# Sparse attention with a fused score step, late normalisation and value products 64 columns wide

## Chip, cores and metric

One NeuronCore of one Trainium2 chip runs the whole program. The metric is the time of one execution on the device, in microseconds. The kernel before was timed three times: 2421.4, 2422.6 and 2425.72 us, median 2422.6 us.

## The reference, cut to what matters

The program is a stack of transformer layers over 256 tokens of width 1024, all in fp32: feed-forward blocks, a convolution mixer, a sparse-attention mixer, and then two further layers with differential and grouped-query attention. The change touches the sparse-attention mixer alone (`nsa_mixer`). It has 16 heads of 64 in 4 groups, and three branches: compressed keys (15 of them), selected blocks and a window. With 256 tokens there are only 4 blocks of 64, and all are selected; the window of 512 holds all keys too. So every branch is a masked softmax over the visible keys, with a distance penalty that has a slope for each head:

```python
def masked_softmax(s, mask):
    s = jnp.where(mask, s, NEG_INF)
    m = jnp.max(s, axis=-1, keepdims=True)
    e = jnp.where(mask, jnp.exp(s - m), 0.0)
    return e / jnp.maximum(jnp.sum(e, axis=-1, keepdims=True), 1e-30)

s = jnp.einsum('bqgrd,bgnd->bgrqn', qb, k_cmp) - sl5 * d_cmp      # likewise for k_sel and kw
p_cmp = masked_softmax(s, d_cmp >= 0)
o_cmp = jnp.einsum('bgrqn,bgnd->bqgrd', p_cmp, v_cmp)
o = gates[0] * o_cmp + gates[1] * o_sel + gates[2] * o_win        # gates = sigmoid(projection)
```

## The kernel before, in words

Each engine has one hand-ordered program, and semaphores join them. Large weight matrices are split into a high and a low fp32r part (`split`, L636 and L1027) and multiplied in three passes. The sparse-attention mixer comes as one of eleven stages, between two feed-forward stages. It has three parts. First four weight units give the queries (`cols_product`) and a narrow one the gates. Then comes the attention loop. Then `down` (L1599) multiplies the result `mid[:, 0:2048]` by the output matrix, in four steps, each of which needs a slice of the result that `mid_split` has split in two (L648 on ScalarE, L1035 on VectorE).

The attention loop runs over `nsa_jobs` (L257): 24 jobs, for each of 4 groups `g`, each of 2 tiles `tt` of 128 queries, and the branches 1, 2 and 0 in that order. A job treats 4 heads together. Its number of keys `nk` is 128 for tile 0 and 256 for tile 1, and 15 in branch 0. Two successive tiles of one group make six jobs, called a pair of tiles below. A job passes through these steps, where J is the loop's step on each engine:

- TensorE, `nsa_pe` (L1739): scores of job J (L1767, 4 products, each two fp32 instructions), into banks 0 and 1 or 2 and 3; transposes of the probabilities of job J-2 (L1779), into bank 4 and, for 256 keys, bank 5; value products of job J-3 (L1789, L1792): the values are the stationary operand, the transposed probabilities of all 4 heads the moving one, 512 columns. The three branches add up in one bank.
- VectorE, `nsa_dve` (L1234): for job J the biased scores (L1256, one instruction for each head), their maximum (L1259), its negation (L1261); then for job J-1 the denominator (L1272 and L1274 only in branch 0, L1276), its reciprocal (L1278), times the gate (L1281), and the product of all probabilities with it (L1284).
- ScalarE, `nsa_act` (L811): the exponentials of job J (L827, one for each head, each with a sum that is read out by a second instruction), the copy of job J-2's transposed probabilities from the banks to `pT` (L835, L838), and for a finished tile the copy of the output (L845, L846).

The probabilities have two buffers, `probs[J % 2]`, and the transposes have one set of banks. VectorE's L1256 of job J waits for the transposes of job J-2 (L1252), which wait for L1284 of job J-2 and for the copy of job J-3. At the loop's end TensorE waits for the last output copies (L1795, L1796).

## Time and profile before

| | |
|---|---|
| median of three executions | 2422.6 us |
| the profiled execution | 2424.26 us |
| its span, first to last instruction | 2422.3 us |
| TensorE busy | 92% of the span |
| VectorE busy | 49% |
| ScalarE busy | 39% |
| mean granted TensorE clock | 0.948 of 2.4 GHz |
| attention loop, first score to first product of `down` | 968.6 to 1109.6 us |

Shares of the whole span are means over eleven stages. The loop is some 6% of the span, and has to be read by itself: with the busy times of a stretch, with the waits in it, and with the chain of work. "Idle before" is the time for which an engine stood still ahead of an instruction, and the name behind the arrow is what released it. A granted clock of 1.00 is 2.4 GHz, and 0.50 is 1.2 GHz.

### The profile page before, as it was taken

The page shows a single profiled execution, that of the slowest core. Times are in us where ns is not written, and L with a number is a line of the kernel's source. Part 1 is how long each engine was busy: PE and PEld are TensorE (multiplying, and loading weights), DVE is VectorE, ACT ScalarE, POOL GpSimd, SP SyncE. Part 2 cuts the span into 40 slices and gives each one's busy share as a digit, 9 for nine tenths or more (in the row PEclk, how much of TensorE's full clock was granted, in tenths as well). Part 3 has the DMA queues.
Part 4 walks back from the last instruction along what each step waited for, and adds up shares of the span by engine and source line. Part 5 has one row for each costly group of instructions (what it writes and reads, how often), then busy time and mean ns, then how long its engine had stood idle before and what let it go on. Part 6 is the DMA issues. An engine that isn't in the chain of part 4 may idle for free.

```text
span 2422.3 us, 34862 instructions
## 1 busy us (share of the span) xinstructions
PE 2228.2 (92%) x14142; PEld 1868.5 (77%) x14142; DVE 1189.1 (49%) x1891; ACT 947.1 (39%) x1456; POOL 92.3 (4%) x140
## 2 busy tenths in 40 slices
PE   4999998999889998677999999788999999898999
PEld 2998786997789978335997799556877768786997
DVE  2344655445724455555445564785222233765454
ACT  2334424334523344445334543564222222455343
POOL 1000000000100000000000100002000000200000
PEclk7999998999969998678999999999999999999999
DMA  7876686767548674003776432002554333225553
GB/s 264 289 252 258 212 319 224 272 227 261 174 160 289 216 273 135 8 1 122 257 251 240 130 105 88 18 2 87 173 174 156 121 139 113 70 70 173 173 176 121
DMA packets 246601, 411.38 MB, mean 170 GB/s; under 512 B 10221, under 2 KB 191942, under 8 KB 246470
## 3 DMA queue, kind: packets, MB, share of 16 engines
q1 hardware_dynamic: 246470, 409.54, 48.8%
q8 instruction: 93, 1.52, 0.3%
q14 instruction: 38, 0.31, 0.0%
HBM read 408.47 MB, written 1.05 MB: 169 GB/s over the span
## 4 chain that ended last, share of the span: by engine, by line
PE 79%; DVE 9%; ACT 5%; DMA 3%; issue 2%; POOL 2%; SPq 0%; DVEq 0%; ACTq 0%; POOLq 0%
PE bank L1629 19%; PE bank L1577 14%; PE bank L1578 13%; PE bank L1579 13%; PE bank L1552 4%; PE bank L1686 3%; PE bank L1688 3%; PE bank L1687 3%; DMA ada<-in_ada_w 2%; ACT gate_b L827 1%; PE bank L1779 1%; PE bank L1720 1%; PE bank L1563 1%; PE bank L1597 1%; DVE astat L1373 1%
## 5 line engine op out<-in xcount | busy, mean ns | idle before, releaser
L1033 DVE TENSOR_TENSOR w_lo<-stage,w_hi 128x2048 fp32r<-128x2048 f32 x255 | 585.8, 2299 | 736.3 <-ACT w_hi L646 736.1
L1577 PE MATMUL bank<-h_hi,w_hi 128*128 128x256 f32 (+1 forms) x2432 | 742.9, 305 | 26.9 <-POOL h_lo L611 20.8
L1578 PE MATMUL bank<-h_lo,w_hi 128*128 128x256 f32 (+1 forms) x2432 | 733.5, 302 | 0.0
L1579 PE MATMUL bank<-h_hi,w_lo 128*128 128x256 f32 (+1 forms) x2432 | 733.2, 301 | 0.0
L646 ACT CAST w_hi<-stage 128x2048 fp32r<-128x2048 f32 x255 | 484.7, 1902 | 620.5 <-PE bank L1579 260.6
L1577 PEld LDWEIGHTS bank<-h_hi,w_hi 128*128 128x128 f32 x2432 | 473.4, 195 | 86.4 <-issue 69.5
L1578 PEld LDWEIGHTS bank<-h_lo,w_hi 128*128 128x128 f32 x2432 | 473.6, 195 | 14.7 <-issue 1.2
L1579 PEld LDWEIGHTS bank<-h_hi,w_lo 128*128 128x128 f32 x2432 | 472.9, 194 | 14.2
L1629 PE MATMUL bank<-w_hi,h_hi 128*128 128x512 f32 x776 | 245.0, 393 | 11.4 <-DVE h_lo L1042 8.0
L1629 PE MATMUL bank<-w_lo,h_hi 128*128 128x512 f32 x776 | 243.2, 390 | 0.0
L1629 PE MATMUL bank<-w_hi,h_lo 128*128 128x512 f32 x776 | 242.7, 390 | 0.0
L981 ACT ACTIVATE silu_t<-bank 128x256 f32<-128x256 f32 (+1 forms) x132 | 54.8, 419 | 340.1 <-PE bank L1579 340.1
L1629 PEld LDWEIGHTS bank<-w_hi,h_hi 128*128 128x128 f32 x776 | 144.1, 188 | 49.4 <-issue 14.6
L1686 PE MATMUL bank<-w_hi,h_hi 128*128 128x256 f32 (+1 forms) x560 | 163.0, 291 | 8.8 <-issue 8.0
L1629 PEld LDWEIGHTS bank<-w_hi,h_lo 128*128 128x128 f32 x776 | 146.1, 188 | 30.7
L1629 PEld LDWEIGHTS bank<-w_lo,h_hi 128*128 128x128 f32 x776 | 146.1, 188 | 30.7
L1688 PE MATMUL bank<-w_hi,h_lo 128*128 128x256 f32 (+1 forms) x560 | 161.3, 288 | 0.0
L1687 PE MATMUL bank<-w_lo,h_hi 128*128 128x256 f32 (+1 forms) x560 | 161.1, 288 | 0.0
L1552 PE MATMUL bank<-ada,cond 128*32 128x512 f32 x1024 | 130.9, 625 | 15.0 <-DMA ada<-in_ada_w 13.6
L1686 PEld LDWEIGHTS bank<-w_hi,h_hi 128*128 128x128 f32 x560 | 110.7, 198 | 10.4 <-issue 9.4
L1452 DVE TENSOR_TENSOR mid<-silu_t,bank 128x256 f32 (+3 forms) x132 | 60.8, 463 | 116.6 <-PE bank L1579 116.6
L1687 PEld LDWEIGHTS bank<-w_lo,h_hi 128*128 128x128 f32 x560 | 110.7, 198 | 0.0
(187 smaller groups left out, 1892.2 us busy)
## 6 DMA issues: line engine op xcount, KB each, us to landing
ada<-in_ada_w SPq DMA_DIRECT2D x120, 1024.0 KB, 7.1
stage<-in_ffn_w_in SPq DMA_DIRECT2D x88, 1024.0 KB, 6.2
stage<-in_ffn_w_out SPq DMA_DIRECT2D x44, 1024.0 KB, 5.2
stage<-in_ffn_w_gu SPq DMA_DIRECT2D x44, 1024.0 KB, 5.1
stage<-in_ffn_w_down SPq DMA_DIRECT2D x22, 1024.0 KB, 5.1
stage<-in_a_w_in SPq DMA_DIRECT2D x12, 1024.0 KB, 7.7
stage<-in_diff_w_in SPq DMA_DIRECT2D x12, 1024.0 KB, 5.2
ada<-in_kv_ada_w SPq DMA_DIRECT2D x8, 1024.0 KB, 6.7
```

The source lines that it names most:

```text
L646: a.copy(w_hi[:, s, :], stage[:, s, :]).then_inc(hi_done, 1)
L981: a.activation(silu_t[:, q, 0:T], bank[q][:, 0:T], ACT.Silu).then_inc(silu_done, 1)
L1033: v.tensor_tensor(w_lo[:, s, :], stage[:, s, :], w_hi[:, s, :].bitcast(F32), ALU.subtract).then_inc(lo_done, 1)
L1452: v.tensor_tensor(mid[:, bass.ds(o, T)], silu_t[:, q, 0:T], bank[2 + q][:, 0:T], ALU.mult).then_inc(mid_done, 1)
L1552: ins = m.matmul(bank[4][z:z + 32, :], cond[:, b, 2 * q + k, :], ada[:, s, k * D + h * 512:k * D + (h + 1) * 512], start=(q == 0), stop=(q ...
L1577: m.matmul(dst[:, 0:T], wh, h_hi[:, h0:h0 + T], start=(k == ks[0]), stop=False)
L1578: m.matmul(dst[:, 0:T], wh, h_lo[:, h0:h0 + T], start=False, stop=False)
L1579: ins = m.matmul(dst[:, 0:T], wl, h_hi[:, h0:h0 + T], start=False, stop=(k == ks[-1]))
L1629: ins = m.matmul(y_bank(T, tt, h)[:, :], a_[:, r:r + P], w_[:, slot, kc * D + h * 512:kc * D + (h + 1) * 512], start=first and n == 0, sto ...
L1686: m.matmul(dst, h_hi[:, r], w_hi[:, slot, c], start=(k == ks[0]), stop=False)
L1687: m.matmul(dst, h_hi[:, r], w_lo[:, slot, c], start=False, stop=False)
L1688: ins = m.matmul(dst, h_lo[:, r], w_hi[:, slot, c], start=False, stop=(k == ks[-1]))
```

## The change

All of it lies in the sparse-attention stage.

- The query copy scales by a value for each row (`q_scale`, made by 16 small memsets at the kernel's start), 1/8 divided by the head's slope. So a score plus the distance, times minus the slope, is the negated biased score.
- One VectorE instruction for each head adds the distance, multiplies by minus the slope, writes the negated score and gives its minimum. Maximum and negation go. In branch 0 an extra subtraction takes the minimum off.
- The exponential has the scale -1. In branch 0 it is one instruction for all 4 heads, with no sum. The mask product goes; the gate of branch 0 is multiplied by a 0/1 column once.
- The probabilities are transposed unnormalised: the product L1284 goes. TensorE waits for the exponential, no longer for VectorE.
- Value products take the transposed probabilities of one head as the stationary operand and 64 columns of values as the moving one: for each head and each 128 keys two instructions. The output has the queries on the partitions; VectorE multiplies it by the coefficients (128x256), GpSimd adds the second and third branch to the first, TensorE transposes the sum (2 transposes for each tile), and VectorE copies it to `mid`.
- `probs` has four buffers, the statistics eight, the outputs two; the transposes go to banks 4 and 5 in turn (`nsa_slots`), each bank freed by its own copy.
- `mid_split` of step j waits for its own tiles alone. Step 0 of it comes two loop steps later on ScalarE.

```diff
+        nsa_slots = []
+        for J in range(len(nsa_jobs) + 7):
+            if 0 <= J - 2 < len(nsa_jobs):
+                nsa_slots += [("t", J - 2, kt) for kt in range((nsa_jobs[J - 2][3] + P - 1) // P)]
+            if J >= 6 and (J - 6) % 3 == 2:
+                nsa_slots.append(("f", (J - 6) // 3, 0))
...
+            def nsa_pool(tag):
+                for i, (g_, tt, br, nk) in enumerate(nsa_jobs):
+                    if br == 1:
+                        continue
+                    k, c = i // 3, i // 3 * 2 + i % 3 - 1
+                    pool.wait_ge(dve_s, t.at((tag, "omul", i)))
...
+                    t.done(g.tensor_tensor(o_sum[k % 2], o_sum[k % 2], o_add[c % 2], ALU.add), pool_s, (tag, "add", c))
...
 nsa_act:
-                        act.wait_ge(dve_s, t.at((tag, "neg", J)))
-                        for r in range(R):
-                            ins = a.activation(probs[J % 2][:, r, 0:nk], probs[J % 2][:, r, 0:nk], ACT.Exp,
-                                               bias=astat[:, J % 2, 1, r:r + 1], accum_out=astat[:, J % 2, 2, r:r + 1])
+                        act.wait_ge(dve_s, t.at((tag, "bias", J)))
+                        if br == 0:
+                            ins = a.activation(pr[:, :, 0:nk], pr[:, :, 0:nk], ACT.Exp, scale=-1.0)
+                        else:
+                            for r in range(R):
+                                ins = a.activation(pr[:, r, 0:nk], pr[:, r, 0:nk], ACT.Exp, scale=-1.0,
+                                                   bias=n_stat(J, 0)[:, r:r + 1], accum_out=n_stat(J, 1)[:, r:r + 1])
...
+                        if i >= 2:
+                            act.wait_ge(pe_s, t.at((tag, "pv", i - 2)))
+                        for kt in range((nk + P - 1) // P):
+                            n = nsa_slot["t", i, kt]
+                            act.wait_ge(pe_s, t.at((tag, "slot", n)))
+                            t.done(a.copy(pT[i % 2][0:w, kt, :], bank[4 + n % 2][0:w, :]), act_s, (tag, "evac", n))
...
 nsa_dve:
-                        if J >= 2:
-                            dve.wait_ge(pe_s, t.at((tag, "jt", J - 2)))
+                        if J >= 4:
+                            dve.wait_ge(pe_s, t.at((tag, "slot", last_slot(J - 4))))
                         for r in range(R):
-                            ins = v.scalar_tensor_tensor(out=probs[b][:, r, 0:nk], in0=d, scalar=slope, in1=sc, op0=ALU.mult, op1=ALU.add)
-                        t.done(v.reduce_max(astat[:, b, 0, :], probs[b][:, :, 0:nk], AX_X), dve_s, (tag, "max", J))
-                        t.done(v.tensor_scalar(astat[:, b, 1, :], astat[:, b, 0, :], -1.0, None, ALU.mult), dve_s, (tag, "neg", J))
+                            ins = v.tensor_tensor_reduce(out=pr[:, r, 0:nk], in0=sc, in1=d, scale=-slope(g, r), scalar=3.0e38,
+                                                         op0=ALU.add, op1=ALU.min, accum_out=n_stat(J, 0)[:, r:r + 1])
...
-                        t.done(v.tensor_tensor(pr, pr, cf, ALU.mult), dve_s, (tag, "p", i))
+                    if 0 <= J - 4 < len(jobs):
...
+                        t.done(v.tensor_tensor(dst.rearrange("p (r d) -> p r d", r=R),
+                                               bank[6 + i % 2][:, 0:256].rearrange("p (r d) -> p r d", r=R), cf, ALU.mult), dve_s, (tag, "omul", i))
+                    if J >= 7 and (J - 7) % 3 == 2:
...
+                        t.done(v.tensor_copy(o, bank[4 + n % 2][:, 0:256].rearrange("p (c t) -> p c t", c=2)), dve_s, (tag, "evac", n))
...
 nsa_pe:
-                        pe.wait_ge(dve_s, t.at((tag, "p", i)))
-                        if i:
-                            pe.wait_ge(act_s, t.at((tag, "evT", i - 1)))
+                        pe.wait_ge(act_s, t.at((tag, "exp", i)))
...
-                            for kt in range(tt + 1):
-                                ins = m.matmul(ob, vn[:, br - 1, kt, g * DH:(g + 1) * DH], pT[i % 2][:, kt, :],
-                                               start=(br == 1 and kt == 0), stop=False)
+                        pe.wait_ge(act_s, t.at((tag, "evac", last_slot(i))))
+                        if i >= 2:
+                            pe.wait_ge(dve_s, t.at((tag, "omul", i - 2)))
+                        for r in range(R):
+                            for kt in range(n_kt):
+                                vals = vc[0:w, g * DH:(g + 1) * DH] if br == 0 else vn[:, br - 1, kt, g * DH:(g + 1) * DH]
+                                ins = m.matmul(bank[6 + i % 2][:, r * DH:(r + 1) * DH], pT[i % 2][0:w, kt, r * P:(r + 1) * P], vals,
+                                               start=(kt == 0), stop=(kt == n_kt - 1))
+                    if J >= 6 and (J - 6) % 3 == 2:
...
+                        pe.wait_ge(pool_s, t.at((tag, "add", 2 * k + 1)))
+                        free_slot(n)
+                        for c in range(2):
+                            ins = m.transpose(bank[4 + n % 2][:, c * P:(c + 1) * P], o_sum[k % 2][:, c * P:(c + 1) * P], ident[:, :])
+                pe.wait_ge(dve_s, t.at((tag, "evac", len(nsa_slots) - 1)))
```

## Rows read from the trace of the kernel before

**Rows 1.** The page's head: the span.

```profile
span 2422.3 us, 34862 instructions
```

**Rows 2.** Busy time of each engine by stretch: the loop, and the stretch behind it.

```profile
core 0: us, PE busy (x) PEld busy (x) DVE busy (x) ACT busy (x) POOL busy (x), PEclk, DMA share, GB/s
...
968.40:1109.50 141.10, 99.85 (x384) 47.92 (x384) 74.79 (x259) 60.85 (x242) 0.00 (x0) 0.70 0.02 5
1109.50:1150.00 40.50, 32.88 (x147) 25.17 (x148) 23.81 (x51) 23.09 (x42) 5.40 (x7) 0.90 0.51 182
```

**Rows 3.** Waits in the loop: who waited for whom; us in total, times, longest.

```profile
ACT gate_b L827 <- DVE astat L1261: 74.5, 23, 4.6
DVE gate_b L1256 <- PE bank L1779: 53.5, 22, 3.1
...
PE bank L1779 <- ACT mid L838: 18.8, 12, 3.6
```

**Rows 4.** Chain of work in mid-loop, in order of time: start us, us, what.

```profile
1054.69 1.42 DVE gate_b L1256 x4
...
1056.14 1.23 DVE astat L1259
...
1057.60 2.08 ACT gate_b L827 x8
1059.68 0.47 ACT mid L835
...
1060.28 1.95 PE bank L1779 x8
...
1062.33 0.42 DVE gate_b L1256 x4
...
1063.02 0.18 DVE astat L1261
...
1063.23 1.27 ACT gate_b L827 x8
1064.49 0.96 ACT mid L838 x2
...
1067.63 0.89 DVE gate_b L1256 x4
...
1069.47 1.65 ACT gate_b L827 x8
```

**Rows 5.** Groups of instructions in the loop: busy us, mean ns; idle before.

```profile
L1792 PE MATMUL bank<-mid 128*64 128x512 f32 x48 | 34.0, 831 | 0.0
...
L1284 DVE TENSOR_TENSOR gate_b<-gate_b,astat 128x1024 f32<-128x1024 f32 x8 | 9.8, 1224 | 0.3
...
L827 ACT ACTIVATE gate_b<-gate_b,astat 128x15 f32<-128x15 f32 x32 | 9.4, 295 | 19.9 <-DVE astat L1261 19.9
```

**Rows 6.** Groups of VectorE over the whole span.

```profile
L1452 DVE TENSOR_TENSOR mid<-silu_t,bank 128x256 f32<-128x256 f32 x50 | 20.6, 418 | 22.6 <-PE bank L1579 22.6
```

**Rows 7.** Groups of GpSimd over the whole span.

```profile
L611 POOL TENSOR_TENSOR h_lo<-mid,h_hi 128x256 fp32r<-128x256 f32 x27 | 19.1, 736 | 0.4 <-ACT h_hi L713 0.4
```

**Rows 8.** TensorE in order of time, parts of the loop: start, us, instructions merged.

```profile
975.77 2.08 PE L1767 MATMUL bank<-mid 64*128 64x256 f32 x8
978.73 0.63 PE L1779 MATMUL bank<-ident,gate_b 128*128 128x128 f32 x4 [0.88 <-ACT mid L838]
980.29 1.13 PE L1767 MATMUL bank<-mid 64*128 64x256 f32 x8
...
1070.77 0.72 PE L1767 MATMUL bank<-mid 64*128 64x128 f32 x8
...
1074.60 0.62 PE L1767 MATMUL bank<-mid 64*128 64x15 f32 x8
```

**Rows 9.** Busy time by stretch, two short parts of the loop (columns as in rows 2).

```profile
1060.30:1070.30 10.00, 9.68 (x30) 5.05 (x30) 4.88 (x21) 3.68 (x17) 0.00 (x0) 0.50 0.00 0
1070.50:1077.10 6.60, 4.07 (x26) 1.94 (x26) 3.02 (x11) 3.68 (x15) 0.00 (x0) 1.00 0.00 0
```

**Rows 10.** Busy time by stretch inside L1720 (128x128 stationary, 60 moving columns, fp32).

```profile
683.00:690.00 7.00, 7.00 (x35) 7.00 (x35) 0.00 (x0) 0.00 (x0) 0.00 (x0) 0.50 0.44 150
```

More of the change, by code:

```diff
@@ L95, in trace @@
         norm_s = sb("norm_s", [P, 8, 8])
+        q_scale = sb("q_scale", [P, KC])
         w_landed = [sem(f"w_landed{i}") for i in range(RING)]
@@ L408, in trace, with n_stat @@
         qT = mid[:, 2048:4096].rearrange("p (c t) -> p c t", c=KC)
-        probs = [gate_b[:, i, :].rearrange("p (r s) -> p r s", r=R) for i in range(2)]
+        probs = [a.rearrange("p (r s) -> p r s", r=R) for a in
+                 (gate_b[:, 0, :], gate_b[:, 1, :], diag[:, :, :].rearrange("p h d -> p (h d)"),
+                  silu_t[:, :, :].rearrange("p h d -> p (h d)"))]
+        o_sum = [mid[:, o:o + 256] for o in (5120, 5376)]
+        o_add = [mid[:, o:o + 256] for o in (9700, 9956)]
+        def n_stat(J, f):
+            o = J % 8 * 32 + f * 4
+            return ada_row[:, o:o + R]
         pT = [mid[:, o:o + 1024].rearrange("p (k n) -> p k n", k=2) for o in (10240, 4096)]
@@ L661, in mid_split @@
                     act.wait_ge(act_s, t.at((f"s{s['n']}", "evo", 1)))
[L662 to L663 removed]
+                elif s["kind"] == "nsa":
+                    act.wait_ge(dve_s, t.at((f"s{s['n']}", "evac", nsa_slot["f", 2 * j + 1, 0])))
                 elif s["kind"] == "gqa" and j == 0:
@@ L812, in nsa_act @@
                 u = s["u"]
+                act.wait_ge(dve_s, t.at("q_scale"))
                 for n in range(4):
@@ L1243, in nsa_dve @@
                 t.done(v.reciprocal(gsig[:, :, :], gsig[:, :, :]), dve_s, (tag, "gsig"))
+                for tt in range(2):
+                    dve.wait_ge(dve_s, t.at((tag, "gsig")))
+                    ins = v.tensor_scalar(gsig[:, tt, 0:HEADS], gsig[:, tt, 0:HEADS], seen_c[:, tt, 0:1], None, ALU.mult)
+                t.done(ins, dve_s, (tag, "gates"))
                 jobs = nsa_jobs
-                for J in range(len(jobs) + 1):
+                for J in range(len(jobs) + 8):
                     if J < len(jobs):
@@ new lines, in nsa_dve @@
+                    if J >= 7 and (J - 7) % 3 == 2:
+                        k = (J - 7) // 3
+                        g, tt, _, _ = jobs[3 * k]
+                        n = nsa_slot["f", k, 0]
+                        dve.wait_ge(pe_s, t.at((tag, "slot", n)))
+                        o = mid[:, 0:2048].rearrange("p (c t) -> p c t", c=KC)[:, 2 * g:2 * g + 2, tt * P:(tt + 1) * P]
+                        t.done(v.tensor_copy(o, bank[4 + n % 2][:, 0:256].rearrange("p (c t) -> p c t", c=2)), dve_s, (tag, "evac", n))
@@ L1418, in gqa_dve @@
                         t.done(v.tensor_scalar(probs_g[b], probs_g[b], astat[:, b, 3, 0:1], None, ALU.mult), dve_s, (tag, "p", i))
+            for c in range(KC):
+                for half in range(2):
+                    h = 2 * c + half
+                    ins = v.memset(q_scale[64 * half:64 * half + 64, c:c + 1], DH ** -0.5 / slope(h // R, h % R))
+            t.done(ins, dve_s, "q_scale")
             for b in range((ncol + P - 1) // P):
@@ L1758, in nsa_pe, with free_slot @@
                 jobs = nsa_jobs
-                for J in range(len(jobs) + 3):
+                def free_slot(n):
+                    if n >= 2:
+                        pe.wait_ge(dve_s if nsa_slots[n - 2][0] == "f" else act_s, t.at((tag, "evac", n - 2)))
+                for J in range(len(jobs) + 7):
                     if J < len(jobs):
@@ L1778, in nsa_pe @@
                             for r in range(R):
-                                ins = m.transpose(bank[4 + kt][0:w, r * P:(r + 1) * P], probs[i % 2][:, r, kt * P:kt * P + w], ident[:, :])
-                        t.done(ins, pe_s, (tag, "jt", i))
-                    if 0 <= J - 3:
+                                ins = m.transpose(bank[4 + n % 2][0:w, r * P:(r + 1) * P], probs[i % 4][:, r, kt * P:kt * P + w], ident[:, :])
+                            t.done(ins, pe_s, (tag, "slot", n))
+                    if 0 <= J - 3 < len(jobs):
@@ L1782, in nsa_pe @@
                         i = J - 3
                         g, tt, br, nk = jobs[i]
-                        ob = bank[6 + (i // 3) % 2][0:64, :]
-                        if i >= 6 and i % 3 == 0:
-                            pe.wait_ge(act_s, t.at((tag, "evO", i - 4)))
-                        pe.wait_ge(act_s, t.at((tag, "evT", i)))
-                        if br == 0:
-                            ins = m.matmul(ob, vc[0:N_CMP, g * DH:(g + 1) * DH], pT[i % 2][0:N_CMP, 0, :], start=False, stop=True)
-                        else:
-                            for kt in range(tt + 1):
-                                ins = m.matmul(ob, vn[:, br - 1, kt, g * DH:(g + 1) * DH], pT[i % 2][:, kt, :],
-                                               start=(br == 1 and kt == 0), stop=False)
```

89 lines of the change are left out of this document (49 added, 40 removed).

## The prediction

> **What bounds the kernel now.** The change lies in one stage, so I read that stage alone, in this order: busy times by stretch, waits, chain, and then prices. The attention loop takes 141.1 us of a span of 2422.3 us [rows 1, 2]. In it TensorE is busy for 99.9 us, VectorE for 74.8 us and ScalarE for 60.9 us, and the DMA engines are at 2%: nobody is full, the DMA is out of it, and the sum of the three, 235.5 us, is only 1.67 times the stretch. The waits say why: ScalarE's exponentials waited 74.5 us for VectorE's negated maximum, VectorE's next scores waited 53.5 us for transposes, and the transposes 18.8 us for ScalarE's copies [rows 3]. That is a ring of waits. The chain in mid-loop walks it [rows 4]: scores biased (1.42 us), maximum (1.23), exponentials (2.08), copy (0.47), transposes (1.95), and only then the next job's scores, because `probs` has two buffers and the transposes one set of banks. With 24 jobs in 141 us, one job costs 5.9 us, of which each engine works for 2.5 to 4.2 us. So it is the order that binds, and behind it TensorE. Behind the loop `down` starts at once and TensorE is busy for 32.9 of 40.5 us [rows 2]; what the loop gives up comes off the end one for one.
>
> **The ring of waits.** After the change VectorE's scores of job J wait for the transposes of job J-4, and the transposes wait for ScalarE's exponential, a loop step older than before in VectorE's order. Neither closes a ring within a job. What is late next is the busiest engine, so I price each engine for one pair of tiles (six jobs; there are four pairs).
>
> **VectorE.** The maximum (1.23 us at 1024 elements), the negation (0.2, start to start [rows 4]) and the product with the coefficients (1.22 us at 1024 elements [rows 5]) go. Four score instructions take 1.42, 0.89 and 0.42 us for 256, 128 and 15 keys [rows 4]. The new ones do the same stream from the bank plus a minimum; I take the same time for the stream. The three small statistics take 0.2 us each, 0.6. New is the product of the output, 128x256 from a bank, 0.42 us [rows 6], and one copy of that size for each tile. Sums: 2 x (0.89 + 0.6 + 0.42) + 2 x (1.42 + 0.6 + 0.42) + 2 x (0.42 + 0.2 + 0.2 + 0.6 + 0.42) + 2 x 0.42 = 3.8 + 4.9 + 3.7 + 0.8 = 13.2 us. The trace shows no VectorE instruction that also gives a minimum. The nearest row has four ScalarE exponentials of 256 with their sums as eight instructions in 2.08 us, 0.52 us a head, where an exponential of 15 takes 0.295 us by itself [rows 4, 5]. The bounds are 0 and 0.2 us for each head (the price of a small instruction); a gain is excluded, since the stream has the same length. I take 0.1 us: 24 heads-with-minimum in a pair, 2.4 us, so 15.6 us a pair, 62 us in all; with the bounds 53 to 72 us.
>
> **ScalarE.** Eight instructions for four exponentials take 2.08 and 1.65 us (256 and 128 keys), before also 1.27 us for 15 keys, where now one instruction of 60 elements stands, about 0.3 us [rows 4, 5]. A copy of a bank takes 0.48 us [rows 4], 8 in a pair. The output copies go. Sum: 2 x 1.65 + 2 x 2.08 + 2 x 0.3 + 8 x 0.48 = 11.9 us a pair, 48 us in all. The query copies keep their shape; I cost them at nothing, on either side of 0 by less than 1 us.
>
> **TensorE, and its clock.** It has two prices, since the loop runs at either clock level: a stretch at 1.2 GHz in which it is 97% busy, and the next at 2.4 GHz [rows 9]. At 2.4 GHz eight score instructions take 1.13, 0.72 and 0.62 us for 256, 128 and 15 keys, and four transposes 0.63 us; at 1.2 GHz eight scores of 256 take 2.08 us and eight transposes 1.95 us [rows 4, 8]. The other scores I double. The old value products took 34.0 us for the 48 instructions of 512 columns in branches 1 and 2 alone [rows 5]. There are now 64 in a pair, 256 in all, with a 128x128 stationary operand and 64 moving columns. The trace has nearly that shape in L1720, 60 columns: 35 in 7.00 us, 0.20 us each, at 1.2 GHz [rows 10]; at 2.4 GHz I take half, 0.10 us. A pair, at 2.4 GHz: scores 2 x (1.13 + 0.72 + 0.62) = 4.9, transposes 8 x 0.63 = 5.0, values 64 x 0.10 = 6.4, four output transposes 0.6: 16.9 us, 68 us in all. At 1.2 GHz: scores 2 x (2.08 + 1.44 + 1.24) = 9.5, transposes 4 x 1.95 = 7.8, values 12.8, output 1.0: 31.1 us, 124 us in all. So the value products gain nothing at 1.2 GHz; TensorE's gain is that it need not wait.
>
> Which level will hold? For one thing, L1720 is busy without a gap, and the clock was still granted at 0.50 [rows 10]: narrow products keep TensorE occupied and don't bring the clock back. That is a third of the new work. For another, in the loop before the clock rose again behind stretches with wide scores: eight score instructions of 256 took 2.08 us at 975.77 and 1.13 us at 980.29 [rows 8]. The new loop has these closer together. The mean was 0.70 before [rows 2]. I take three pairs at 2.4 GHz and one at 1.2 GHz. The Trainium skill (TensorE: Matmul & The Clock Gate, Part 4: PE-mode transpose) says that transposes don't count as TensorE activity for the clock. The stretch from 1060.3 to 1070.3, in which two sets of eight transposes of 1.95 us each fell, was at 0.50 [rows 4, 9], which agrees but doesn't prove it; by that rule the case at 1.2 GHz (first rival) would be the likelier one.
>
> **GpSimd and the new waits.** 16 additions of 128x256 cost 0.74 us each [rows 7], 12 us on an engine that did nothing in the loop. TensorE's output transposes wait for them; they are placed two loop steps behind VectorE's product, some 6 us, which hides 0.5 us of product and 0.74 of addition. Behind that wait stand TensorE's next scores: if the cover were gone, it would cost 1.2 us for each of 8 tiles. TensorE's value products wait for the output product of two jobs earlier, with the same cover. `q_scale`'s 16 memsets lie at the start, where VectorE waits for data.
>
> **The sum.** At 2.4 GHz the engines need 16.9, 15.6 and 11.9 us a pair. A job with 256 keys is longest on TensorE or ScalarE, one with 15 on VectorE, each engine works in a fixed order and each hand-over costs about 0.1 us, so a pair takes more than its largest; I estimate 19.5 us. Three pairs at 19.5 and one at 31.1 are 90 us. At the end the last job still has to be transposed, multiplied, scaled, added, transposed, copied and split: about 5 us beyond the steady state; the first job needs 1 us. Together 95.5 us against 141.1, a gain of 45.6 us. Of the span of 2422.3 us 2376.7 us remain; with the 2.0 us that lie around it 2378.7 for a profiled execution, which stands 1.7 us above the median. So 2377 us.
>
> **The rivals.**
> First, TensorE stays at 1.2 GHz in the whole loop. For it speaks L1720 [rows 10], against it that scores did bring the clock back before. TensorE is then the bound with 124 us, plus 3 us of hand-overs and 6 us of ends: 133 us, gain 8 us, 2414 us. Mixed cases fill 2400 to 2416.
> Second, all at 2.4 GHz and the engines interlock nearly without loss: 68 us and 5 us of ends, 73 us, gain 68 us, 2355 us. Against it: the fixed orders on three engines of almost equal load.
> Third, the change doesn't do what it says: the loop stays a ring, for instance because ScalarE copies job J-2 only behind the exponentials of job J. Then only the removed links go: 24 times the maximum and the negation (1.23 us at 1024 elements, 0.7 in the mean of the sizes, and 0.2) and 8 times 1.0 us of exponential, 30 us: 2392 us. Against it: no wait that I can name closes a ring within a job.
> Fourth, slower: TensorE at 1.2 GHz throughout, and at each of its waits for a copy or for the output product it stands still, since it must take scores, transposes and values in the written order. With 6 us of ends it decides from the point where such stops add 11 us, 0.5 us for each job, to 124 us; at 1.0 us for each job the loop takes 124 + 24 + 6 = 154 us, 13 us longer, 2436 us. Against it: with TensorE as the bound, copies and products are ready early.
> Fifth, the instruction with the minimum costs much more than 0.2 us extra, say twice its stream: 21.6 us more on VectorE, 84 us in all and about 100 us for the loop, 2382 us, still in the range.
>
> **How the numbers follow.** The forecast has 0.62, TensorE at 1.2 GHz 0.20, the loop without loss 0.06, the ring 0.05, no difference 0.02, slower 0.05. 8 in 10 lie between 2355 and 2415 us: the lower end is the second rival, the upper the first. A measurement of this kernel can tell about 0.2% from no change, 5 us. Faster by more: 0.92; within: 0.03; slower by more: 0.05.
>
> **What would show it.** Right: the wait of the exponentials for VectorE falls from 74.5 us to under 20 us; TensorE is busy for over 80% of the loop; the value products lie 0.10 us apart at 2.4 GHz and 0.20 us at 1.2 GHz; the clock in the loop is above 0.8. Wrong: a loop clock near 0.5 (first rival), score instructions with more than 0.3 us beyond the old ones, or scores that wait for transposes (third). All other stages should keep their times within 1 us.

## The result, and the profile after

The changed kernel takes 2408.0 us (median of 2402.7, 2412.2, 2410.1 and 2405.9), against 2424.1 us for the kernel before in the same comparison: a ratio of 0.9934, 95% interval 0.9909 to 0.9958. The forecast was 2377 us. So the gain is 16 us where 46 were expected; the direction was right and the time lies inside the range, near its upper end. The execution that was profiled is the fastest of the four, 2402.7 us with a span of 2400.7 us; its granted clock over the whole span was 0.943, that of the others 0.939 to 0.940.

Busy time by stretch of the changed kernel: the attention loop, and 40.5 us behind it. The columns are those of [rows 2], which are also the rows of before.

```profile
core 0: us, PE busy (x) PEld busy (x) DVE busy (x) ACT busy (x) POOL busy (x), PEclk, DMA share, GB/s
968.10:1085.80 117.70, 107.48 (x592) 90.17 (x592) 51.10 (x318) 51.78 (x173) 11.61 (x16) 0.62 0.02 6
1085.80:1126.30 40.50, 33.84 (x138) 25.39 (x139) 22.52 (x50) 17.27 (x36) 4.37 (x6) 0.84 0.51 182
```

The loop went from 141.0 to 117.7 us: 23.3 us. It starts 0.5 us earlier, and from its end to the end of the span the kernel is 2.2 us longer than before (1314.9 against 1312.7 us). 23.3 + 0.5 - 2.2 gives the 21.6 us by which the two spans differ. The second row shows a lower clock right behind the loop (0.84, where it was 0.90), but that is not where the 2.2 us went. The changed kernel is 23.8 us ahead at the loop's end, 21.7 us at the first transposes behind `down` (L1588 before, L1647 now: 1137.2 and 1115.5 us), and 23.6 us again at the first L1827 (now L1899: 1399.5 and 1375.9 us). It is 23.1 us ahead at the first L1881 (now L1953: 1620.6 and 1597.5 us), and 21.5 us at the next L1563 (now L1622: 1757.3 and 1735.8 us). Most of what is missing at the end was lost there, some 600 us behind the loop, in stages that the change doesn't touch.

In the loop the reader is to see two things. TensorE is busy for 107.5 of 117.7 us, 91%: it is now the bound. And its clock is 0.62, below the 0.70 of before, though TensorE stands still for 10.2 us of the loop, where it was 41.2 us. A clock of 0.62 means that about a quarter of the time was granted 2.4 GHz and three quarters 1.2 GHz.

The waits in the loop of the changed kernel (who waited for whom; us in total, times, longest), to be set against [rows 3]:

```profile
DVE gate_b L1294 <- PE bank L1832: 24.1, 10, 5.7
ACT gate_b L870 <- DVE ada_row L1294: 23.8, 7, 5.4
ACT silu_t L870 <- DVE ada_row L1294: 15.3, 4, 5.4
DVE silu_t L1294 <- PE bank L1832: 14.0, 5, 5.7
DVE diag L1294 <- PE bank L1832: 11.7, 5, 3.8
DVE mid L1330 <- PE bank L1857: 10.3, 4, 4.6
ACT diag L870 <- DVE ada_row L1294: 9.1, 4, 3.9
```

The four probability buffers go by three names here (`gate_b` holds two). VectorE's scores no longer wait for transposes; they wait 24.1 + 14.0 + 11.7 = 49.8 us for TensorE's scores (L1832), and ScalarE's exponentials (L870) wait 48.2 us behind them. The ring is gone, and everybody queues behind TensorE.

Groups of instructions in the loop of the changed kernel, busy us, mean ns, idle before: the value products (L1857), the scores of 256 keys (L1832), the additions (L654), the output products (L1330), the read-out of the minimum (L1294) and the transposes of the output (L1866).

```profile
L1857 PE MATMUL bank<-mid 128*128 128x64 f32 x192 | 37.2, 372 | 0.4 <-ACT mid L882 0.3
...
L1832 PE MATMUL bank<-mid 64*128 64x256 f32 x64 | 14.3, 589 | 0.0
L1857 PE MATMUL bank<-mid 15*128 15x64 f32 x64 | 13.7, 380 | 0.0
...
L654 POOL TENSOR_TENSOR mid<-mid 128x256 f32<-128x256 f32 x16 | 11.6, 725 | 134.6 <-DVE mid L1330 134.6
...
L1330 DVE TENSOR_TENSOR mid<-bank,ada_row 128x256 f32<-128x256 f32 x24 | 10.2, 424 | 10.3 <-PE bank L1857 10.3
...
L1294 DVE DVE_READ_ACCUMULATOR2_ANT ada_row<- 128x1 f32 x96 | 8.0, 83 | 0.0
...
L1866 PE MATMUL bank<-ident,mid 128*128 128x128 f32 x16 | 5.3, 429 | 0.7 <-POOL mid L654 0.7
```

TensorE in order of time near the end of the loop of the changed kernel: start us, us, instructions merged, idle before.

```profile
1065.49 1.10 PE L1857 MATMUL bank<-mid 128*128 128x64 f32 x8 [0.34 <-ACT mid L882]
1066.53 0.62 PE L1832 MATMUL bank<-mid 64*128 64x15 f32 x8
...
1069.34 1.61 PE L1857 MATMUL bank<-mid 15*128 15x64 f32 x8
1070.88 0.69 PE L1866 MATMUL bank<-ident,mid 128*128 128x128 f32 x2
1071.36 1.92 PE L1844 MATMUL bank<-ident,diag 128*128 128x128 f32 x8
1073.07 3.51 PE L1857 MATMUL bank<-mid 128*128 128x64 f32 x16
1076.37 1.06 PE L1844 MATMUL bank<-ident,silu_t 128*15 128x128 f32 x4
1077.23 5.41 PE L1857 MATMUL bank<-mid 128*128 128x64 f32 x24
1082.57 0.69 PE L1866 MATMUL bank<-ident,mid 128*128 128x128 f32 x2
```

From start to start, eight value products take 1.04 us at 2.4 GHz (1065.49 to 1066.53, 0.13 us each), and 16 take 3.30 us at 1.2 GHz (0.21 us each). From 1070.9 to 1082.5 us TensorE is never without work, and it is at 1.2 GHz throughout. The row at 1069.34 is no price at either level, since the clock fell inside it: it is 0.96 from 1069.34 to 1069.80 us and 0.50 from there on.

### The profile page after: what moved, and what is told of

Read it like the earlier page. It is cut to its first block, busy times and chain, and to the rows that moved or that the text cites. A ratio compares the mean times of both kernels' runs of the same rounds, so it can differ in the third digit from the quotient of the medians.

```text
span 2400.7 us, 35371 instructions
## 1 busy us (share of the span) xinstructions
PE 2237.5 (93%) x14350; PEld 1910.9 (80%) x14350; DVE 1165.9 (49%) x1965; ACT 934.9 (39%) x1384; POOL 103.9 (4%) x156
## 4 chain that ended last, share of the span: by engine, by line
PE 82%; DVE 8%; DMA 3%; ACT 3%; issue 2%; POOL 2%; SPq 0%; DVEq 0%; ACTq 0%; POOLq 0%
PE bank L1688 20%; PE bank L1636 14%; PE bank L1637 13%; PE bank L1638 13%; PE bank L1611 4%; PE bank L1745 3%; PE bank L1747 3%; PE bank L1746 3%; PE bank L1857 2%; DMA ada<-in_ada_w 2%; PE bank L1779 1%; PE bank L1622 1%; DVE astat L1427 1%; PE bank L1832 1%; PE bank L1656 1%
```

## The experiments

All totals are medians of several executions, with the ratio to the kernel before and its interval. Loop figures are those of the profiled execution, so they can differ from the total by several us. Idle products and transposes are added work whose results nobody reads. The question was why the clock is 0.62, and what each part of the change is worth in a loop that hangs on it.

**1. Value products wide again.** The changed kernel with the values as stationary operand and 512 moving columns.

```diff
-for r in range(R):
-    for kt in range(n_kt):
-        ins = m.matmul(bank[6 + i % 2][:, r * DH:(r + 1) * DH], pT[i % 2][0:w, kt, r * P:(r + 1) * P], vals, ...)
+for kt in range(n_kt):
+    ins = m.matmul(bank[6 + i % 2][0:64, :], vals, pT[i % 2][0:w, kt, :], ...)
```

> The changed kernel with one edit: the value products in the form of the kernel before, values stationary, 512 moving columns, 64 instructions in place of 256. What is left out: the products land on 64 partitions, so what follows scales and adds the wrong layout. The price on TensorE is nearly the same at either clock level: 64 times 0.43 us against 256 times 0.10 us at 2.4 GHz, 64 times 0.85 against 256 times 0.20 us at 1.2 GHz. Theory (the narrow products keep the clock at 1.2 GHz, and TensorE at that level bounds the loop): the mean granted clock in the loop rises from 0.62 to 0.85 or more and the loop falls from 118 us to 85 to 95 us, total 2375 to 2385 us. Rival (the fixed orders of three engines and the hand-overs bind): clock and loop stay within 5 us of 118 us, total 2400 to 2410 us.

Measured: 2377.3 us, 0.9817 (0.9793 to 0.9840). The loop of this kernel, as a stretch:

```profile
965.10:1055.50 90.40, 77.68 (x401) 37.95 (x401) 50.68 (x318) 51.54 (x173) 11.62 (x16) 0.92 0.01 5
```

The scores of 256 keys in it, which the edit doesn't touch:

```profile
L1832 PE MATMUL bank<-mid 64*128 64x256 f32 x64 | 10.0, 436 | 0.0
```

The theory's clock, loop and total were all met. One edit takes the clock from 0.62 to 0.92 and the loop from 117.7 to 90.4 us, near the 95.5 of the forecast. Of the 27.3 us, some 17 lie in instructions that stayed as they were: the groups of scores, transposes and output transposes add up to 46.9 us, where they were 63.9. But the edit also takes away instructions, so it doesn't say yet whether their number or their width did it.

**2. More work for TensorE.** The changed kernel with two idle fp32r products of 256 columns ahead of each head's value products, 192 in all.

```diff
 for r in range(R):
+    for _ in range(2):
+        m.matmul(bank[6 + i % 2][:, 256:512], h_hi[:, 2048:2176], h_hi[:, 2048:2304], start=True, stop=True)
```

> The changed kernel with work added: 192 fp32r products of 256 columns into the unused half of the output banks, two ahead of each head's value products. They cost TensorE 20 us at 2.4 GHz or 41 us at 1.2 GHz. Theory (narrow products keep the clock low): the denser stream brings the clock to 0.9 or more, and the loop takes 95 to 110 us, no longer than without them, total 2390 to 2405 us. Rival (the clock does not hang on the width of what is multiplied, TensorE is simply the bound): the loop grows by 25 to 40 us to 143 to 158 us, total 2430 to 2445 us.

Measured: 2409.1 us, 0.9942 (0.9922 to 0.9963).

```profile
968.80:1090.50 121.70, 113.14 (x784) 95.62 (x784) 50.93 (x318) 51.74 (x173) 11.65 (x16) 0.86 0.01 4
```

Neither expectation was met: the theory had a clock of 0.9 and a loop of 95 to 110 us, the rival 143 to 158 us. 192 more instructions cost the loop 4.0 us, and the medians of the total are 1 us apart, within their spread. The clock rose to 0.86, and the old work became faster by about as much as the new work takes. So it isn't the amount of work that keeps the clock down.

**3. Narrow value products in the kernel before.**

```diff
-ins = m.matmul(ob, vn[...], pT[i % 2][:, kt, :], ...)
+for r in range(R):
+    ins = m.matmul(bank[6 + (i // 3) % 2][:, r * DH:(r + 1) * DH], pT[i % 2][0:w, kt, r * P:(r + 1) * P], vals, ...)
```

> The kernel before with one part of the change alone: value products with 64 moving columns, 256 instructions. What is left out: the three branches are not added up and the output copies take the wrong layout. Theory: the clock in the loop falls from 0.70 to 0.6 or less, and the loop, a ring of waits in which transposes and scores lie, takes 5 to 15 us longer than 141 us, total 2428 to 2438 us. Rival (the shape is neutral, as its price at a given clock says): 141 us within 4 us, total 2420 to 2428 us.

Measured: 2431.4 us, 1.0028 (1.0014 to 1.0043).

```profile
966.90:1115.20 148.30, 117.69 (x577) 101.92 (x577) 74.72 (x259) 60.95 (x242) 0.00 (x0) 0.51 0.01 3
```

The same edit the other way round, in a loop that is still a ring: the clock falls from 0.70 to 0.51, that is to 1.2 GHz nearly throughout, and the loop gets 7.3 us longer. This is what the theory had.

**4. Rings of four and the fused minimum, with the old way of multiplying.** The probabilities are normalised ahead of the transposes, and the value products are 512 wide and add up in one bank; the rest is the change. GpSimd has no part in the loop.

```diff
+cf = n_stat(i, 4).unsqueeze(2).broadcast_to([P, R, nk])
+t.done(v.tensor_tensor(pr, pr, cf, ALU.mult), dve_s, (tag, "p", i))
...
+ins = m.matmul(ob, vals, pT[i % 2][0:w, kt, :], start=(br == 1 and kt == 0), stop=(br == 0))
```

> A complete kernel: rings of four, two alternating transpose banks, fused minimum and negated scores as in the change, but the probabilities multiplied by the coefficients before the transposes and the value products 512 wide with the sum over branches in the bank, as in the kernel before; no work on GpSimd, no output transposes. VectorE has 8 us more than in the change, TensorE 2 us less. Theory: clock 0.85 or more in the loop, loop 80 to 95 us, total 2365 to 2380 us. Rival (order and hand-overs bind): the loop stays at 110 to 125 us, total 2400 to 2412 us.

Measured: 2364.4 us, 0.9758 (0.9734 to 0.9782), the fastest of all.

```profile
967.40:1048.20 80.80, 72.50 (x384) 36.59 (x384) 55.08 (x309) 53.49 (x186) 0.00 (x0) 0.92 0.03 9
```

It computes all that the reference asks for, and it is 44 us faster than the changed kernel. Clock and loop are in the theory's ranges, the total just below its 2365 us. VectorE has 4.0 us more to do (the product with the coefficients costs more on 512 or 1024 elements than on 256), TensorE 35 us less.

**5. More work for VectorE.** The changed kernel with the product of the output done twice.

```diff
+t.done(v.tensor_tensor(dst..., bank[6 + i % 2][:, 0:256]..., cf, ALU.mult), dve_s, (tag, "extra", i))
+dve.wait_ge(dve_s, t.at((tag, "extra", i)))
 t.done(v.tensor_tensor(dst..., bank[6 + i % 2][:, 0:256]..., cf, ALU.mult), dve_s, (tag, "omul", i))
```

> The changed kernel with VectorE's output product done twice in each job: 24 more instructions of 0.42 us and their hand-overs, 11 us more on VectorE, nothing else changed. Theory (TensorE at 1.2 GHz bounds the loop, VectorE is busy 51 of 118 us): the loop stays within 3 us, total 2403 to 2413 us. Rival (the fixed order of the three engines binds, VectorE's part of it included): the loop grows by 8 to 11 us, total 2416 to 2421 us.

Measured: 2400.1 us (2393.3 to 2411.9), 0.9902 (0.9866 to 0.9938).

```profile
963.70:1087.00 123.30, 111.37 (x593) 93.48 (x593) 60.67 (x342) 51.85 (x173) 11.59 (x16) 0.60 0.03 9
```

VectorE is busy for 9.6 us more. Neither expectation was met: the loop of the profiled execution is 5.6 us longer (the theory had 3 at most, the rival 8 to 11), while the median of the total is 8 us shorter, with executions 19 us apart. That the added 9.6 us show in full in the total is excluded; a few us either way can't be read from it. So VectorE is not the bound of the whole loop; whether it costs a part of it stays open.

**6. Two probability buffers in experiment 4.**

```diff
-pr = probs[J % 4]
+pr = probs[J % 2]
...
-if J >= 4:
-    dve.wait_ge(pe_s, t.at((tag, "slot", last_slot(J - 4))))
+if J >= 2:
+    dve.wait_ge(pe_s, t.at((tag, "slot", last_slot(J - 2))))
```

> The complete kernel of e4 (normalised, wide values, 80.8 us for the loop) with two buffers for the probabilities in place of four, so that VectorE's scores of job J wait for the transposes of job J-2 again. Theory (the ring of waits was the main cost of the kernel before, the fused minimum a lesser one): the loop takes 105 to 120 us, total 2388 to 2405 us. Rival (the ring mattered little, the gain is from the removed VectorE work): 81 to 90 us, total 2364 to 2374 us.

Measured: 2382.6 us, 0.9824 (0.9807 to 0.9841). The loop, and VectorE's wait for transposes, its largest:

```profile
970.60:1070.40 99.80, 80.77 (x385) 39.45 (x385) 56.26 (x309) 52.84 (x186) 0.00 (x0) 0.85 0.02 8
```

```profile
DVE gate_b L1297 <- PE bank L1827: 31.3, 22, 2.5
```

L1827 are the transposes: the wait that led [rows 3] for VectorE is back, 31.3 us, and costs 19.0 us of loop (99.8 against 80.8). The ring was real, and the four buffers remove it. The loop is shorter than the theory had it (105 to 120 us) and longer than the rival did (81 to 90 us).

**7. Transposes as ordinary products.** The changed kernel; each transpose of probabilities becomes an fp32 product with the identity, which is two instructions.

```diff
-ins = m.transpose(bank[4 + n % 2][...], probs[i % 4][:, r, kt * P:kt * P + w], ident[:, :])
+ins = m.matmul(bank[4 + n % 2][...], probs[i % 4][:, r, kt * P:kt * P + w], ident[:, :], start=True, stop=True)
```

> The changed kernel with its 128 transposes issued as ordinary fp32 products with the identity, 256 instructions, 14 us more on TensorE at 2.4 GHz, 27 us at 1.2 GHz. If transposes did not count for the clock (a page of the Trainium skill, TensorE: Matmul & The Clock Gate, says so), now they would: the clock in the loop rises from 0.62 to over 0.85 and the loop takes 95 to 112 us in spite of the work, total 2385 to 2402 us. If transposes count like other products of 128 columns, the stream is hardly denser: clock 0.6 to 0.7, loop 130 to 145 us, total 2420 to 2435 us.

Measured: 2380.4 us, 0.9809 (0.9792 to 0.9825). The loop, and the value products in it (128 rows and, in branch 0, 15):

```profile
967.70:1064.90 97.20, 89.87 (x721) 77.18 (x721) 51.14 (x318) 51.96 (x173) 11.59 (x16) 0.94 0.02 8
```

```profile
L1857 PE MATMUL bank<-mid 128*128 128x64 f32 x192 | 24.0, 275 | 0.0
...
L1857 PE MATMUL bank<-mid 15*128 15x64 f32 x64 | 8.8, 277 | 0.0
```

128 more instructions, a clock of 0.94, and a loop 20.5 us shorter: the narrow products, left as they were, take 24.0 us in place of 37.2. Clock and loop are as the theory had them, and the total is below its range by 5 us. The Trainium skill (TensorE: Matmul & The Clock Gate, Part 4: PE-mode transpose) says that the full clock doesn't engage for transposes, since they don't count as busy time in the same way. This run's clock, 0.94 for 0.62, agrees with it. But the edit also doubles the number of these instructions, so it can't tell their mode from their number. I held the rule for the cause until experiment 11.

**8. The rings alone.** Before's arithmetic (maximum, negation, normalised probabilities, wide values) with four buffers, two transpose banks in turn, and each step of `down` waiting for its own tiles only; the mask product is gone.

```diff
-pr = probs[J % 2]
+pr = probs[J % 4]
...
-bank[4 + kt]
+bank[4 + n % 2]
```

> The kernel before with the rings alone: four probability buffers, two transpose banks in turn, separate statistics, and each down step waiting for its own tiles; scores, maximum, negation, exponentials and normalisation as before, without the mask product. VectorE has 20 us more than e4 (75 against 55 us), ScalarE 8 us more. Theory (the ring of waits was the main cost): the loop takes 88 to 100 us, total 2372 to 2385 us. Rival (the fused minimum is what helped): 115 to 130 us, total 2398 to 2413 us.

Measured: 2388.4 us, 0.9846 (0.9829 to 0.9862).

```profile
970.40:1074.00 103.60, 85.02 (x384) 42.26 (x384) 72.39 (x253) 60.89 (x242) 0.00 (x0) 0.80 0.02 7
```

Both expectations missed (88 to 100 us, and 115 to 130): the ring and the fused minimum each matter. This splits the change. The rings with what goes with them are worth 37.4 us of loop (141.0 to 103.6). The fused minimum with its cheaper exponentials is worth 22.8 us more (103.6 to 80.8, experiment 4). The rest of the change, narrow products on unnormalised probabilities with their output product, additions and transposes, gives 36.9 us back (80.8 to 117.7). Each of these sizes holds what the clock did along with it (0.70, 0.80, 0.92, 0.62). The medians of the totals, 2424.1, 2388.4, 2364.4 and 2408.0 us, give the same split: 36, 24 and -44 us.

**9. Experiment 7's edit in the fastest kernel.**

```diff
-ins = m.transpose(bank[4 + n % 2][...], probs[i % 4][:, r, kt * P:kt * P + w], ident[:, :])
+ins = m.matmul(bank[4 + n % 2][...], probs[i % 4][:, r, kt * P:kt * P + w], ident[:, :], start=True, stop=True)
```

> The version with wide values and probabilities normalised ahead of the transposes (loop 80.8 us, clock 0.92, total 2364.4 us), with its 128 transposes of probabilities issued as ordinary fp32 products with the identity: 256 instructions in their place. Theory (the transposes keep the granted clock down): the clock is 0.92 already, so there is little left to win; the loop clock goes to 0.98 or more, TensorE works some 3 to 5 us longer, and the loop stays between 78 and 84 us, the total between 2360 and 2369 us. Rival (ordinary products are simply the faster form of the transpose, whatever the clock): the loop shortens again by some 15 us or more, as it did in the changed kernel with its narrow products, and the total falls below 2352 us.

Measured: 2373.5 us, 0.9789 (0.9763 to 0.9815).

```profile
970.00:1061.00 91.00, 85.08 (x512) 51.24 (x512) 54.98 (x309) 54.45 (x186) 0.00 (x0) 0.95 0.02 8
```

The value products in it, to be set against those of experiment 7:

```profile
L1840 PE MATMUL bank<-mid 128*64 128x512 f32 x48 | 24.0, 609 | 0.0
...
L1840 PE MATMUL bank<-mid 15*64 15x512 f32 x16 | 8.5, 612 | 0.0
```

Both missed. The clock had little left to gain, but the doubled instructions cost 12.6 us of TensorE and 10.2 us of loop, not 3 to 5. Ordinary products are the dearer form of a transpose; here they pay only through the clock. The rows show one thing more: at clocks of 0.95 and 0.94 all wide value products take 32.5 us and all narrow ones 32.8 us. At nearly one clock the two forms cost the same.

**10. The same edit in the kernel before.** The edit is that of experiment 9, at L1779.

> The kernel before with its transposes of the probabilities issued as ordinary fp32 products with the identity, nothing else. Theory (transposes keep the granted clock down, and the loop of before is a ring of waits): the loop clock rises from 0.70 to over 0.90; since TensorE's share of each turn of the ring (scores and transposes) shrinks where it ran at 1.2 GHz, the loop shortens by 8 to 20 us, to 121 to 133 us, and the total to 2405 to 2416 us. Rival one (the clock follows TensorE's busy share, and the ring sets that): the clock stays at 0.65 to 0.75, each transpose now costs two instructions, and the loop gets 2 to 8 us longer, 2426 to 2433 us. Rival two (the clock rises but VectorE and ScalarE set the ring): the loop is within 3 us of 141, the total within 5 us of before.

Measured: 2447.6 us, 1.0097 (1.0074 to 1.0120). The loop, VectorE's wait for transposes in it, and one set of transposes in order of time:

```profile
969.90:1135.40 165.50, 120.89 (x513) 72.93 (x513) 74.64 (x259) 60.93 (x242) 0.00 (x0) 0.70 0.01 4
```

```profile
DVE gate_b L1256 <- PE bank L1779: 75.8, 22, 4.9
```

```profile
1036.30 3.75 PE L1779 MATMUL bank<-ident,gate_b 128*128 128x128 f32 x16 [3.05 <-ACT mid L835]
```

The clock stays at 0.70 to the digit. Rival one had that and the sign, but not the size: 24.5 us, where it had 2 to 8. The price at 1.2 GHz sits on the ring (16 instructions in 3.75 us, where before eight transposes took 1.95 [rows 4]), and VectorE's wait for transposes grew by 22.3 us, from 53.5 [rows 3] to 75.8. A theory in which the transposes alone hold the clock down can't explain a clock that doesn't move when they go. TensorE stood idle for 44.6 us of this loop; that, too, may keep its clock low, which no run here separates.

**11. Idle transposes.** If transposes are what starves the clock, more of them must not help.

```diff
 for r in range(R):
+    m.transpose(bank[6 + i % 2][:, 256:384], ident[:, :], ident[:, :])
```

> The changed kernel with one idle transposition ahead of each head's value products: the identity transposed into an unused part of the output's bank, 96 in all. At the prices of the loop (a transpose takes 0.24 us at 1.2 GHz and 0.16 us at 2.4 GHz) that is 15 to 23 us more work on TensorE, which is 91% busy. Theory (transposes don't help the clock): the loop clock stays at 0.50 to 0.62, and the whole work shows: loop 133 to 145 us, total 2420 to 2435 us. Rival (any instruction that occupies TensorE helps the clock, as the filler of wide products did, whose 192 instructions raised it from 0.62 to 0.86): the loop clock goes over 0.75, and the loop stays between 112 and 125 us, the total between 2396 and 2412 us.

Measured: 2395.4 us (2391.9 to 2404.0), 0.9894 (0.9867 to 0.9922).

```profile
969.50:1078.90 109.40, 99.03 (x688) 81.13 (x689) 50.64 (x318) 51.73 (x173) 11.63 (x16) 0.83 0.01 4
```

The theory fell. 96 transposes that serve nothing raised the clock from 0.62 to 0.83, and the loop got 8.3 us shorter. The clock over the whole span says the same of every execution: 0.949 to 0.956, against 0.939 to 0.943 without them. The rival had the clock, while its loop (112 to 125 us) was a little too long. Against the Trainium skill's rule on transposes this run speaks as plainly as experiment 7 seemed to speak for it.

**12 and 13. Idle ordinary products, 128 or 64 columns wide.** Same places as in experiment 11, the same stationary operand, 192 instructions each; between the two only the moving columns differ.

```diff
 for r in range(R):
+    m.matmul(bank[6 + i % 2][:, 256:384], ident[:, :], ident[:, :], start=True, stop=True)      # 12
+    m.matmul(bank[6 + i % 2][:, 256:320], ident[:, :], ident[:, 0:64], start=True, stop=True)   # 13
```

> The same 96 idle transpositions of the identity in the same places, each issued as an ordinary fp32 product of the identity with the identity (two instructions of 128 columns, 192 in all). Operands, place and result are the same; only the mode differs. At 2.4 GHz such a pair takes about 0.28 us, so this is 27 us more work, and more at 1.2 GHz. Theory (ordinary products help the clock, transposes don't): the loop clock goes to 0.80 or more, and the loop to 105 to 125 us, shorter than with the idle transposes although the added work is larger; total 2390 to 2412 us. Rival (mode makes no difference): the loop clock is within 0.05 of that with the idle transposes; by the added work the loop is then longer than with them by 5 to 25 us.

> The kernel with 96 idle products of the identity (192 instructions), with 64 moving columns in place of 128: same places, same stationary operand, same count, half the columns. With 128 columns the loop took 119.3 us at a clock of 0.89. Theory (instructions with 64 moving columns occupy TensorE without keeping its clock up): the clock stays at 0.50 to 0.68, each added instruction costs about 0.19 us, 37 us in all, and the loop takes 140 to 160 us, over 20 us longer than with twice the columns; total 2430 to 2450 us. Rival (any added work raises the clock): the clock is 0.80 or more, and with less work than at 128 columns the loop takes 105 to 119 us, total 2390 to 2407 us.

Measured for 128 columns: 2407.2 us, 0.9934 (0.9914 to 0.9955).

```profile
968.20:1087.50 119.30, 110.03 (x785) 93.25 (x785) 51.01 (x318) 51.76 (x173) 11.62 (x16) 0.89 0.02 6
```

Measured for 64 columns: 2449.5 us, 1.0113 (1.0093 to 1.0133). The loop, and the idle products in it:

```profile
965.20:1131.60 166.40, 158.61 (x785) 137.13 (x785) 51.17 (x318) 52.08 (x173) 11.59 (x16) 0.56 0.02 7
```

```profile
L1854 PE MATMUL bank<-ident 128*128 128x64 f32 x188 | 53.5, 384 | 0.0
```

Half the columns, and the loop is 47 us longer. With 128 columns the clock is 0.89, with 64 it is 0.56, while TensorE is busy for 92% and 95% of the loop. The last theory's clock was met; its loop (140 to 160 us) was passed by 6.4 us. And the expectation of experiment 12 that ordinary products would give a shorter loop than idle transposes failed: 119.3 against 109.4 us, 9.9 us longer with the larger work, as its rival had it. The clocks, 0.89 and 0.83, are 0.06 apart, where the rival had 0.05 at most. So idle transposes raise the clock nearly as far as idle products of the same columns do, while 64 columns in place of 128 take the rise away.

## Why the prediction was right or wrong

**Right: the ring, and what takes its place.** Experiment 8 shows 37.4 us for removing it, experiment 6 shows 19.0 us for the buffers alone in the fast loop. That TensorE is late next, and that it is busy for over 80% of the loop, is in the row of after (91%). The third rival is out.

**Wrong, the step that failed: "I take three pairs at 2.4 GHz and one at 1.2 GHz".** As a mean over 58.5 and 31.1 us that is a clock of 0.83; the loop had 0.62. With a quarter of the time at 2.4 GHz and three quarters at 1.2, my two prices (68 and 124 us) give 1 / (0.24 / 68 + 0.76 / 124) = 104 us of TensorE, where the forecast's mix gave 3 x 16.9 + 31.1 = 82. The loop missed by 117.7 - 95.5 = 22.2 us, and that this is the same 22 us is in part luck. TensorE was busy for 107.5 us, 26 more than the 82, and it stood still for 10.2 us, 3.5 less than the sum allowed (95.5 - 81.8 = 13.7). The mechanism stood in the prediction: narrow products "keep TensorE occupied and don't bring the clock back" [rows 10]. I then let the wide scores of [rows 8] outweigh it. Experiments 1 and 3 show that narrow value products in place of wide ones lower the clock in both loops (0.92 to 0.62, 0.70 to 0.51), and 12 and 13 that the columns do it at an equal number of instructions. Narrow products alone don't fix the level: experiments 2, 7, 11 and 12 keep all 256 of them, add wider work, and have 0.83 to 0.94. I also called them a third of the new work; by my own prices they are 12.8 of 31.1 us at 1.2 GHz, 41%.

**A row read by the wrong feature.** I took from [rows 8] that scores of 256 columns bring the clock back. In the changed kernel these scores run as often as before and in less time, and the clock is lower. What the row didn't show was what else the loop held: 64 value products of 512 columns (the 48 of [rows 5] and 16 of branch 0), which the change removes. They were the widest work of the old loop, and experiment 1, which puts them back, has a clock of 0.92.

**The Trainium skill's rule on transposes.** I weighed it and left it out of the sum. Experiment 7 (0.94) agrees with it, experiments 10 (0.70, as before) and 11 (0.83) don't. The stretch that I set beside it, at 0.50 [rows 9], couldn't tell: it held two sets of transposes, but also six value products of 512 columns, for some 5 of its 10 us:

```profile
1062.15 1.97 PE L1789 MATMUL bank<-mid 15*64 15x512 f32 x2
...
1067.46 3.38 PE L1792 MATMUL bank<-mid 128*64 128x512 f32 x4
```

By the Trainium skill's rule the first rival would have been likelier, and the loop lies between the forecast and that rival; but that would have been right for a reason that the runs don't bear out.

**TensorE's prices.** At 1.2 GHz the value products came 0.21 us apart (forecast 0.20), at 2.4 GHz 0.13 (forecast 0.10, half of a row at the other level). In experiment 7, at 0.94, 192 take 24.0 us, 0.125 us each. Halving the row at the other level was wrong: for 256 products it is 8 us too little in the case without 1.2 GHz.

**VectorE.** Forecast 62 us, measured 51.1. The instruction with the minimum costs nothing beyond its stream: the heads start 0.34 to 0.35 us apart at 256 keys, before (1.42 - 0.42) / 3 = 0.33 us [rows 4], and the 83 ns of the read-out lie under the start of the next. That is 96 x 0.1 = 9.6 us of the 11 us. The fifth rival is out. The output product took 0.424 us (0.42). Two heads of one job, start and us:

```profile
1065.01 0.42 DVE L1294 CUSTOM_DVE_ANT_0 diag<-bank,mid 128x256 f32<-128x256 f32 x1
1065.36 0.08 DVE L1294 DVE_READ_ACCUMULATOR2_ANT ada_row<- 128x1 f32 x1
1065.36 0.42 DVE L1294 CUSTOM_DVE_ANT_0 diag<-bank,mid 128x256 f32<-128x256 f32 x1
```

**ScalarE and GpSimd.** 51.8 us against 48; additions of 0.725 us against 0.74, 11.6 us in all, and TensorE waited 0.7 us for them in the whole loop, at its very end. The cover held everywhere else.

**The signs named.** The exponentials' wait fell to 48.2 us, not under 20: with TensorE as the bound they wait for scores that come late. "Loop clock near 0.5" was the sign of the first rival, above 0.8 that of the forecast; it came out in between, and so did the time. The other stages did not keep within 1 us: together they took 2.2 us more behind the loop, and the lead fell from 23.1 to 21.5 us far behind it. No run here shows why.

**The total.** In the profiled pair the gain is 21.5 us (2424.3 to 2402.7), in the medians 16.1. The executions of the changed kernel spread over 9.5 us with clocks of 0.939 to 0.943; where in them the slower ones lost their time is open, since one of each was profiled. The forecast took a profiled execution to stand 1.7 us above the median; this one stood 5.3 us below its own.

## What to carry to other kernels

Price TensorE work at both clock levels, and ask of each rewritten product not only how long it is but whether it is wide: a rewrite that moves fewer columns over a full stationary operand can lose more by the clock of everything around it than its arithmetic gains. Take a change of many parts apart before keeping it whole; here two parts were worth 60 us of loop and the third gave 37 back; the kernel of experiment 4 keeps only the first two. When a rule seems to explain a clock, add more of the suspect: if the clock rises, it wasn't that.

## What the runs showed of the hardware

- A busy TensorE isn't enough for 2.4 GHz. With 192 idle fp32 products of 128 columns TensorE was busy for 92% of the loop at a clock of 0.89; with 64 columns in their place, for 95% at 0.56. The share of time in which weights are loaded doesn't order the clocks either: it is 77% of the changed loop (0.62), 79% in experiment 7 (0.94), 78% in experiment 12 (0.89) and 82% in experiment 13 (0.56).
- At nearly one clock narrow and wide value products cost the same: 256 of 64 columns take 24.0 + 8.8 = 32.8 us at 0.94, and 64 of 512 columns 24.0 + 8.5 = 32.5 us at 0.95. What the width changed was the clock.
- Idle work can shorten a loop: 96 idle transposes took it from 117.7 to 109.4 us. In the totals this is 2395.4 against 2408.0 us, with intervals against before (0.9867 to 0.9922, 0.9909 to 0.9958) that just overlap, so the gain is less sure than the rise of the clock.
- A transpose issued as an ordinary fp32 product takes twice the instructions: 16 in 3.75 us at 1.2 GHz for what eight transposes did in 1.95.
- Products over 15 rows aren't cheaper than those over 128: in experiment 7, at 0.94, 64 take 8.8 us (0.14 us each) and 192 over 128 rows take 24.0 us (0.125 us each).
- A VectorE instruction that also gives a minimum over its row costs nothing over its stream, at 256 keys: starts 0.34 to 0.35 us apart, where they were 0.33 without it.
- What is open: by what the clock is decided. The runs order the cases; they give no rule that would forecast 0.62 rather than 0.55 or 0.70.
